# A two-layer hybrid attention block: another order of the transposes in the loop over attention heads

## The reference, cut to what matters

```python
def attend(q_nope, q_rope, k_nope, k_rope, v):
    s = einsum('bqhd,bkhd->bhqk', q_nope, k_nope) + einsum('bqhr,bkr->bhqk', q_rope, k_rope)
    p = softmax(s.astype(float32), axis=-1)
    o = einsum('bhqk,bkhd->bqhd', p, v)
...
q = (rmsnorm(q_lat, qc_g) @ w_q_up)       # per head: 128 plain + 64 rotated
q_nope = rmsnorm(q[..., :NOPE_DIM], qn_g) ; k_nope = rmsnorm(kv[..., :NOPE_DIM], kn_g)
q_rope = rope(rmsnorm(q[..., NOPE_DIM:], qr_g))
```

## Time and profile before

| | |
|---|---|
| median of three runs | 1566.22 us |
| the profiled execution's own time | 1565.72 us |
| its span | 1563.9 us |
| PE busy | 1455.2 us (93%) |
| DVE busy | 1051.0 us (67%) |
| ACT busy | 530.7 us (34%) |
| POOL busy | 71.6 us (5%) |
| mean granted TensorE clock | 0.976 of full speed |

### The profile page before, as it was taken

How to read it: one execution, slowest core, us unless ns; L and a number is a source line. 1 busy time by engine, 2 the same in 40 slices (tenths; PEclk the granted TensorE clock), 3 DMA queues, 4 the chain that set the end, 5 groups by cost and what they waited for, 6 DMA issues and landing times.

```text
span 1563.9 us, 20695 instructions
## 1 busy us (share of the span) xinstructions
PE 1455.2 (93%) x7750; PEld 1231.5 (79%) x7750; DVE 1051.0 (67%) x1549; ACT 530.7 (34%) x783; POOL 71.6 (5%) x107
## 2 busy tenths in 40 slices
PE   3897889997999999999999997988897999999999
PEld 1686777786888888888888886876775888888887
DVE  4588887688986666657566678667756555556555
ACT  3341465423322221222212124455533423232232
POOL 0023110000000000000000000320000000000000
PEclk9899999998999999999999998999998999999999
DMA  8343100152454332433334321310011323323234
GB/s 340 128 144 134 36 8 9 68 175 81 139 183 148 108 118 88 130 123 115 100 105 134 121 68 52 106 49 8 0 54 54 108 81 107 98 92 105 80 107 134
DMA packets 44554, 157.90 MB, mean 101 GB/s; under 512 B 5344, under 2 KB 6752, under 8 KB 43744
## 3 DMA queue, kind: packets, MB, share of 16 engines
q1 hardware_dynamic: 44512, 157.35, 30.6%
HBM read 155.23 MB, written 2.10 MB: 101 GB/s over the span
## 4 chain that ended last, share of the span: by engine, by line
PE 76%; DVE 15%; issue 3%; ACT 2%; DMA 2%; POOL 0%; SPq 0%; DVEq 0%; ACTq 0%; POOLq 0%
PE ps L589 63%; PE ps L544 4%; DVE ada_out L1132 3%; PE ps L546 3%; PE ps L545 3%; DVE w_lo L1117 2%; DVE qkt L1357 1%; DVE tmp L1203 1%; DVE ss L1179 1%; DVE prob L1404 1%; DMA ada_step<-in_w_step 1%; PE ps L720 1%; DVE pt_lo L1219 1%; PE ps L558 1%; DVE H_lo L1211 1%
## 5 line engine op out<-in xcount | busy, mean ns | idle before, releaser
L589 PE MATMUL ps<-H_hi,w_hi 128*128 128x512 f32 (+1 forms) x1248 | 383.6, 357 | 20.8 <-DVE H_lo L1211 12.4
L589 PE MATMUL ps<-H_hi,w_lo 128*128 128x512 f32 (+1 forms) x1248 | 385.5, 359 | 0.0
L589 PE MATMUL ps<-H_lo,w_hi 128*128 128x512 f32 (+1 forms) x1248 | 383.4, 357 | 0.0
L861 ACT ACTIVATE w_hi<-w_raw 128x1024 fp32r<-128x1024 f32 x174 | 181.3, 1055 | 498.3 <-PE ps L589 471.1
L589 PEld LDWEIGHTS ps<-H_hi,w_hi 128*128 128x128 f32 x1248 | 210.3, 190 | 59.4 <-issue 22.5
L1226 DVE SCALAR_TENSOR_TENSOR X<-ps,mod,X 128x512 f32<-128x512 f32 (+3 forms) x288 | 178.8, 656 | 116.2 <-PE ps L589 116.2
L1117 DVE TENSOR_TENSOR w_lo<-w_raw,w_hi 128x1024 fp32r<-128x1024 f32 x174 | 214.3, 1242 | 38.9 <-ACT w_hi L861 36.0
L589 PEld LDWEIGHTS ps<-H_hi,w_lo 128*128 128x128 f32 x1248 | 209.5, 190 | 34.7
L589 PEld LDWEIGHTS ps<-H_lo,w_hi 128*128 128x128 f32 x1248 | 208.4, 189 | 35.4
L1498 DVE SCALAR_TENSOR_TENSOR tmp<-ps,vec,tmp 128x511 f32<-128x511 f32 (+1 forms) x132 | 87.2, 661 | 140.5 <-ACT tmp L1087 132.1
L1132 DVE SCALAR_TENSOR_TENSOR ada_out<-ada_raw,cb 128x1024 f32<-128x1024 f32 x131 | 164.6, 1256 | 13.8 <-ACT cb L901 4.3
(11 more groups left out here) (177 smaller groups left out, 1844.2 us busy)
## 6 DMA issues: line engine op xcount, KB each, us to landing
w_raw<-in_w_main SPq DMA_DIRECT2D x176, 512.0 KB, 3.3
ada_raw<-in_w_ada SPq DMA_DIRECT2D x85, 512.0 KB, 4.0
ada_step<-in_w_step SPq DMA_DIRECT2D x4, 2048.0 KB, 15.7
hw_raw<-in_w_head SPq DMA_DIRECT2D x8, 320.0 KB, 2.9
X<-in_x SPq DMA_DIRECT2D x2, 1024.0 KB, 7.0
cb<-in_cvec SPq DMA_DIRECT2D x2, 1024.0 KB, 5.7
out_x<-X SPq DMA_DIRECT2D x8, 256.0 KB, 4.7
rtab<-in_rope SPq DMA_DIRECT2D x4, 384.0 KB, 5.8
```

The lines of the kernel that those rows point to most:

```text
L589: ins = pe.matmul(job.ps(a, b), ww[:, wsl], xx[:, xk, a:b], start=first and n == 0, stop=last and n == 2)
L861: act.activation(w_hi[c % 4][:], w_raw[c % 2][:], ACT.Copy).then_inc(chunk_hi, 1)
```

## The change

The order in the loop over heads is changed on TensorE, ScalarE and VectorE. Before: transposes of q, k, T0, rotated q, T1, values 0, T2, values 1, T3, values 2, values 3. Now: T0, q, T1, k, values 0, rotated q, T2, values 1, T3, values 2, values 3. With it go the numbers of the PSUM jobs: T0 from 9 to 7, q from 7 to 8, T1 from 11 to 9, k from 8 to 10, the attention output from 13 to 11, rotated q still after its turn but as 12 instead of 10, T2 from 12 to 13, T3 and `b_v` as before (14 and 15). So in slot 3 stand now the token product 3, T0 (7), the attention output (11) and `b_v` (15), where it was 3, q (7), T1 (11) and `b_v` (15); the attention output was in slot 1. The last head of a layer and everything outside the loop keep their order.

```diff
-    J_S, J_B, J_BT, J_T, J_PV, J_V, J_HEAD = (0, 1, 5, 6), 2, (7, 8, 10), (9, 11, 12, 14), 13, 15, 16
+    J_S, J_B, J_BT, J_T, J_PV, J_V, J_HEAD = (0, 1, 5, 6), 2, (8, 10, 12), (7, 9, 13, 14), 11, 15, 16
...
                 turn(0)
                 if between:
-                    between()
+                    between(0)
                 turn(1)
+                if between:
+                    between(1)
                 values(0)
+                if between:
+                    between(2)
                 turn(2)
                 values(1)
                 turn(3)
...
-                for n in range(2):
-                    b_turn(n, j0 + J_B, j0 + J_BT[n], h, J_HEAD, h + 1)
                 attend([j0 + x for x in J_T], j0 + J_PV, h, J_HEAD, h,
-                       lambda: b_turn(2, j0 + J_B, j0 + J_BT[2], h, J_HEAD, h + 1))
+                       lambda n: b_turn(n, j0 + J_B, j0 + J_BT[n], h, J_HEAD, h + 1))
...
-                for n in range(2):
-                    b_half(n, j0 + J_BT[n], h, J_HEAD)
-                attend([j0 + x for x in J_T], h, J_HEAD, h, 1,
-                       lambda n: b_half(2, j0 + J_BT[2], h, J_HEAD))
+                attend([j0 + x for x in J_T], h, J_HEAD, h, 3,
+                       lambda n: b_half(n, j0 + J_BT[n], h, J_HEAD))
...
-                b_half(0, j0 + J_BT[0], h, J_HEAD, h + 1)
-                attend([j0 + x for x in J_T], h, J_HEAD, h, 2,
-                       lambda n: b_half(n + 1, j0 + J_BT[n + 1], h, J_HEAD, h + 1))
+                attend([j0 + x for x in J_T], h, J_HEAD, h, 3,
+                       lambda n: b_half(n, j0 + J_BT[n], h, J_HEAD, h + 1))
```

## The result

The changed kernel takes 1607.02 us (four runs, 1604.81 to 1607.62) against 1564.81 of before: a ratio of 1.0273, interval 1.0236 to 1.0309. The forecast was 1592, 1579 to 1603: the sign was right, the size 15 us short. The profiled execution took 1604.81 us with a span of 1603.0. The ratios in this document are of fast runs, and the only slow one is an execution of version 3 (8272.92 us, cause unknown), without which the median of version 3 is 1582.0 us instead of 1582.3.

A forecast was written before the change was run, and what follows sets the result against it. The untouched feed-forward matmuls have 63%, so only the six head-loop turns counted, with TensorE waiting on VectorE. 15.6 us at full clock plus 10.5 of clock falls made 26.1 over 1566.2: 1592 us, range 1579 to 1603.

The forecast's parts named there:

- T0 gains nothing: T0's last transposes wait for `prob` in either order, so starting T0 earlier gains 0.
- The work behind T0 and the new wait at full clock: Later work behind T0 plus TensorE's wait for `cat_a_lo` before `b_v`: 9.3 us in layer 0, 6.3 in layer 1.
- The wait alone: TensorE waits before `b_v` until `cat_a_lo` has read slot 3: 2.3 us a turn in layer 0, 1.8 in layer 1.
- what stands behind T0: Transposes, halves and last values behind T0 come later: 0.8 us a turn in layer 0, 0.3 in layer 1.
- VectorE's idle time before T1's and T2's halves: Sign to look for in the profile after: VectorE has no idle time before these halves.
- A fall behind T0's hole in every turn: TensorE's clock halves behind the hole between scores and last probabilities: 1.9 us each, 11.4 in six turns.
- Six falls: One clock fall a turn, behind T0: 11.4 us, or 10.5 less the 0.9 the third turn already has.
- a rival with a chance of 0.18: Clock falls twice a turn, also at the wait before `b_v`: 1.8 us more each, 1603 us; chance 0.18.
- The clock rule: Half rate is TensorE's default and only sustained activity releases it; by it all six turns fall.

The follow-up runs named there:

- version 3: Changed kernel with dummy transposes in both holes of a turn: 20 before T0's last probabilities, 16 (12 in layer 1) before `b_v`; 1582.28 us, ratio 1.01 to before.
- version 5: Changed kernel with dummy transposes only in the wait before `b_v`, T0's hole left empty; 1593.87 us, ratio 1.0178 to the kernel before.
- version 2: Kernel before with one wait added: TensorE waits for the last reading of the attention output before `b_v`; 1594.39 us, ratio 1.0171 to the kernel before.
- Version 6: Changed order with the attention output in slot 1 (no wait before `b_v`) and 20 dummy transposes ahead of T0; 1573.1 us, ratio 1.0032 to before.
- version 9: Kernel before with dummy transposes before probabilities (6 a turn; 4, 8, 5 in last heads) and around later norms (24 before, 34 behind); 1552.67 us, ratio 0.9925.

## Why the prediction was wrong

**T0 gains nothing: right.** Its last pair waits 0.83 us for `prob`, as before.

**The work behind T0 and the new wait at full clock, 15.6 us: right.** With both holes filled the change costs 1582.3 - 1566.3 = 16 us, with one fall of 3.4 us left in the turns of either kernel. By parts: a turn of that kernel lasts 34.65 us in layer 0 and 30.36 in layer 1, 3.4 and 2.1 more than before, where 3.1 and 2.1 were said. The wait alone cost 2.4 and 1.9 a turn (said: 2.3 and 1.8), what stands behind T0 34.65 - 33.62 = 1.0 and 0.2 (said: 0.8 and 0.3). VectorE's idle time before T1's and T2's halves did not vanish as announced (0.38 and 2.16 us in the changed kernel's first turn), where TensorE is at half rate. At full clock, in the second turn of version 3, the first did vanish and 0.97 us of the second stayed: T2's transposes start at 242.08 us, right behind VectorE's last reading of T1's slot, as the forecast had it.

**A fall behind T0's hole in every turn, 11.4 us: right.** Measured with the wait filled: 11.6. That the two agree so well is in part luck: the 11.6 is what filling T0's hole saved, with one short fall left over, and the executions of version 5 alone spread over 6 us (1588.82 to 1594.84).

**The step that failed: "Six falls".** The forecast counted one fall a turn, and put the falls behind the new wait at nothing. The wait before `b_v` is a second hole with a fall behind it, five times in six. I had this as a rival with a chance of 0.18, and against it the argument that the value products around the wait are dense. They are, but TensorE's busy share just before and in the wait (1.08 of 3.2 us in version 2, 2.83 of 5.0 in the changed kernel) was enough to bring the clock down, and `b_v` with the scores behind it is TensorE's densest work of the turn, where half rate costs most. The wait's falls cost 16.9 us in the old order, 20.6 in the new one with T0's hole filled, and 13.1 on top of T0's falls (24.7 - 11.6). The rival's price, 1.8 each or 11 in all, was also low: the fall lasted up to 6.8 us there, and I had priced the 3.4 us of the third turn. The terms of the forecast so corrected, 15.6 + 11.6 + 13.1 - 0.9 = 39.4, come close to what the two traces show, 1603.0 - 1563.9 = 39.1 (the medians differ by 42.2). This tests the 15.6 alone, since 11.6 and 13.1 are together, by their making, what filling both holes took off.

**The clock rule.** The page "TensorE: Matmul & The Clock Gate" of the Trainium skill ("What's actually happening") has full rate follow sustained activity, and by it I said that all six turns fall. They do. The same rule applied to the hole that the change itself makes would have given the second set of falls; I applied it in the sum only to the hole that the kernel had, and left the other to a rival.

**What stays open.** The two sets of falls cost 7.5 us less together than apart, and an estimated 5 of them are time at 0.50 that is missing behind the wait when T0's hole is empty too; why the falls there are shorter then, and why the second turn of layer 0 has none, is not shown. Nor is it shown why one fall stays in the first turn when T0's hole is filled. Version 6 does not settle whether the order alone costs 3.3 us, 5 or 7.4. And nothing here explains why the feed-forward matmuls of two executions ran 8.9 us shorter at the same clock; executions of one kernel scatter by over 10 us (1554.21 to 1568.55 for before), and this may be a part of it. Differences of a few us between medians of four executions are to be read with that in mind; the 42 us are not in doubt, since the traces before and after both take 496.0 us there.

## What to carry to other kernels

Six waits of about 2 us on TensorE, with dense matmuls behind them, cost 11.8 us by themselves and 16.9 more by the clock here: price each hole that a change makes or widens by what follows it at half rate. When a job moves to another buffer, list for every buffer who now follows whom; here the numbers in one table put `b_v`, and with it the whole next turn, behind the last reading of the turn. Where a hole can't be removed, transposes of the identity into columns that are overwritten can keep the clock up; look at the granted clock afterwards, for in one turn of version 3 twenty of them did not. And before a gain is put down to an edit, compare the stretches that the edit does not touch: 8.9 of the 12.2 us between the traces of version 9 and the kernel before lay there.

## What the runs showed of the hardware that I had not expected

The clock fell although TensorE was not idle: with 2.83 busy of 5.0 us around the wait, while before it had stayed at 1.00 with 2.93 of 5.3. It came back only after 3.4 or 6.8 us, in the longer case in spite of 6.50 busy of 6.5 us. And useless work paid for itself: 20 and 16 transposes a turn (12 for the 16 in layer 1) took 24.7 us off the changed kernel. Last, the granted clock does not tell all: at 1.00 and with TensorE never idle, the same feed-forward matmuls took 496.0 us in nine traces and 487.2 in two.
